# Stream turns moved from the first gate pass to the output stage; ScalarE evicts queries ahead of the Gelu

## The chip, the core and the metric

The kernel runs on one core of a Trainium2 chip, in float32. The metric is the device time of one execution in microseconds (us), lower is better.

## The reference, cut to what matters

One layer of a hybrid encoder over 384 tokens: a prompt of 256 (two tiles of 128) and eight running streams of 16 tokens, which make one tile.

```python
xn = rmsnorm(x)                                  # (tokens, 2048)
qA, kA, vA, qB, kB, vB, f, gA, gB = split(xn @ w_in)
m  = sigmoid(gA) * (yA @ w_br_a) + sigmoid(gB) * (yB @ w_br_b)   # yA, yB: two attentions
h  = x + m @ w_out
q  = rmsnorm(h) @ w_pq                           # 8 heads x 2 halves x 128
s  = q . sub_keys                                # 128 scores for each half
# top 16 of each half, top 16 of their 256 sums -> 128 experts of a token, idx and gate
a  = peer_u[idx] . rmsnorm(h)                    # a row of 2048 floats for each expert
y  = h + sum(gelu(a) * gate * peer_v[idx])       # and another such row
```

With 128 experts of each token, a tile of 128 tokens needs 128 gathers of 128 rows from `peer_u`, 1 MB each, and as many from `peer_v`.

## The kernel before

**Two fronts.** The part up to the scores s is a front. The streams' front runs first, then the prompt's; while the prompt's front runs (TensorE works for it), the streams' experts are worked off beside it on GpSimd (gathers) and VectorE (arithmetic).

**Stream turns.** The streams' 128 experts are 32 turns of 4 slots, and a half is 2 slots. For each slot `expert_turn` makes a dot with a gathered row of `peer_u` (L1490) and adds the row of `peer_v` that belongs to the slot one turn earlier (L1480). Between two turns stands a Gelu on ScalarE (L877) and a small product with the gates (L1471), which waits for it. The rows of u have 2 buffers, those of v have 4: GpSimd issues the next gather (L492) when the dot or the add has freed a buffer. The 64 halves are dealt out by hand along the prompt's front: `HALVES` in its attention groups, `PASS_HALVES` in its four gate passes (so many before the pass's products, so many behind them), one behind each of four output chunks and two behind the root, and `QUERY_HALVES` in the four query chunks. ScalarE runs the same deal, since its Gelus lie in its own program between the front's evictions.

**The prompt's front behind its attention.** A gate pass i is three chunks of weights (gate A, gate B, branches), a chunk being 4 pieces of 1 MB in a ring of four buffers (`wring`); the gates of pass 0 have been multiplied already within the last attention group, so that pass 0 holds the branches alone. VectorE multiplies gates and branches (L1311) and adds the two (L1316), TensorE turns the result (L756), and the next pass begins. The output stage is four chunks of `w_out`: VectorE adds x and scales (L1326, L1333), TensorE turns it (L773) behind the next chunk. Then comes the root of the second norm: ScalarE squares (L1020), places the last turned chunk (L1011) and takes the square root (L871), and VectorE finishes rstd and writes `xn2` (L1338), the normed h that the prompt's dots will read. The query stage is four chunks of `w_pq`; its first two pieces are multiplied before the last turn of h. For each chunk, ScalarE evicts it with rstd as scale (L1048), runs the Gelus of `QUERY_HALVES`, places the turned queries (L1033) and evicts the key scores (L1038).

**Picking.** `pick` finds a prompt tile's experts in four parts of 9 steps (top 8 twice of both halves, sums, top 8 twice, places, two lookups, name) and a finish. Part i of the first tile needs the scores of query chunk i, and the first 32 gathers of the tile need part 0. Before the change three steps follow each slot of the third query turn and of the last four adds (`last_rows`), which makes 24; the rest lies between the prompt's dots, two steps for each nine dots.

**The prompt's experts.** GpSimd gathers 256 u-tiles into six buffers, of which two lie outside the weight ring and four are the ring's (L533); VectorE makes 256 dots (L1541). Behind them the first halves of the v rows are worked off by dense products on TensorE and the second halves by gathers.

SP loads all weight pieces in order: a piece is issued when TensorE is through with the one that lay in its buffer (`piece_done`).

Of the kernel before, what the change touches and what calls it, by code (L numbers as in the profile page):

```python
# [18 lines left out]
NCH = D // CW  # L19
# [11 lines left out]
TURN = 4  # L31
# [10 lines left out]
PASS_HALVES = (4, 3)  # L42
# [145 lines left out]
def build(nc, a):  # L188

    with ExitStack() as ctx:  # L190
# [201 lines left out]
        def _(pool):  # L392
# [132 lines left out]
            for k in range(2 * SLOTS):  # L525
# [3 lines left out]
                if k == 2:  # L529
                    pool.wait_ge(R.pq_read, 2 * NCH)  # L530
# [334 lines left out]
        def _(act):  # L865
# [35 lines left out]
            def front(F, experts):  # L901
# [91 lines left out]
                for i in range(NCH):  # L993
                    for s in range(2):
# [5 lines left out]
                        experts(PASS_HALVES[0] // 2)  # L1000
# [4 lines left out]
                    experts(PASS_HALVES[1])  # L1005
# [8 lines left out]
                for i in range(NCH):  # L1014
                    if i:
                        place_h(i - 1)
                    experts(1)
# [7 lines left out]
                experts(2)  # L1025

                def keys(i):
                    for t in range(n):
                        u = n * i + t
                        act.wait_ge(F.pq_turned, u + 1)  # L1030
                        if i:
                            act.wait_ge(F.key_done, n * i)
                        act.activation(F.pqT[:, :, t * P:(t + 1) * P], blocks(6 + u % 2), ACT.Copy  # L1033
                                       ).then_inc(F.pq_placed, 1)
                    for t in range(n):
# [6 lines left out]
                for i in range(NCH):  # L1042
                    act.wait_ge(piece_done, F.after(PQ + i))
                    for t in range(n):
                        if i:
                            act.wait_ge(F.pq_turned, n * (i - 1) + t + 1)
                        act.wait_ge(F.xn2_ready, t + 1)
                        act.activation(stage[:, t, :], ps[:, 2 * (i % 2) + t, :], ACT.Copy,  # L1048
                                       scale=rstd[:, 1, t0 + t:t0 + t + 1]).then_inc(F.pq_read, 1)
                    experts(QUERY_HALVES[i])  # L1050
                    keys(i)
# [100 lines left out]
        def _(dve):  # L1152
# [53 lines left out]
            def front(F, experts, between=None):  # L1206
# [99 lines left out]
                for i in range(NCH):  # L1306
                    experts(PASS_HALVES[0])
# [11 lines left out]
                    experts(PASS_HALVES[1])  # L1319

                dve.wait_ge(F.x_again, 16)
                for i in range(NCH):
# [159 lines left out]
            def expert_turn(E, tau, xn, h, first=False, slots=range(TURN), between=None):  # L1482
# [4 lines left out]
                for s in slots:  # L1487
# [6 lines left out]
                    if between:  # L1494
                        between()
# [19 lines left out]
            def stream_turns(halves, between=None):  # L1515

                for tau, half in streams_place.next(halves):
                    expert_turn(ES, tau, S.xn2[:, 0, :], S.h[:, 0, :], first=streams_place.first(tau),
                                slots=range(half * TURN // 2, (half + 1) * TURN // 2), between=between)
# [5 lines left out]
            def pick_steps():  # L1525

                for _ in range(3):
                    stages.pop(0)()

            front(R, stream_turns, pick_steps)  # L1530
# [44 lines left out]
            for k in range(2 * SLOTS):  # L1575
                dot(k)
                if k == SLOTS + 1:
# [97 lines left out]
```

## Time and profile before

| what | us |
|---|---|
| median of 3 runs | 2933.37 (2932.15 to 2935.93) |
| the profiled execution, its own time | 2943.72 |
| its span in the trace | 2941.8 |
| VectorE busy | 1909.7 |
| TensorE busy (matmul) | 2120.5 |
| DMA moved | 1047.10 MB, mean 356 GB/s |

The profiled execution is 10.35 us over the median of the runs, and 1.9 us of it lie outside the span. Times of the trace below are in us from the start of the span. The prompt's gate passes end at about 1437, its output stage at 1563, its query stage at 1713; the dots begin at 1737 and end at 2403.

### The profile page before, as it was taken

The numbers are of one execution on the slowest core, as the hardware profiler recorded it, in microseconds if no ns is written. First come the engines' busy times: TensorE is split into PE (matmuls) and PEld (weight loads), VectorE is DVE, ScalarE is ACT, GpSimd is POOL, SyncE is SP. The second block draws the span as 40 slices with busy tenths as digits, with TensorE's granted clock in tenths as the row PEclk, the third lists the DMA queues.
The fourth block names the chain that finished last, engine by engine and source line by source line (L and its number), as shares of the span: only waits on it lengthen the run. The fifth ranks groups of instructions, "written<-read, shape, count | busy, mean of one in ns | idle before, by whom it ended". The sixth has DMA issues, their size and how long they took to land.

```text
span 2941.8 us, 19523 instructions
## 1 busy us (share of the span) xinstructions
PE 2120.5 (72%) x6070; PEld 1074.1 (37%) x6070; DVE 1909.7 (65%) x2627; ACT 470.9 (16%) x1104; POOL 1241.2 (42%) x854
## 2 busy tenths in 40 slices
PE   7999999999999978878888820000232027999997
PEld 3665444444545533333334410000231015444443
DVE  1212000276686877557545799999999998666666
ACT  1212100112222211001001000000795025000000
POOL 2000000014253455335324437777777875444444
PEclk9999999999999989989999965555555557999998
DMA  9777688869799999899988969999999997999999
GB/s 356 265 287 256 230 285 300 300 222 397 287 405 372 407 412 411 340 401 362 395 315 352 409 247 396 397 400 398 393 402 400 413 377 246 409 408 407 409 409 361
DMA packets 271464, 1047.10 MB, mean 356 GB/s; under 512 B 19856, under 2 KB 19856, under 8 KB 203280
## 3 DMA queue, kind: packets, MB, share of 16 engines
q0 software_dynamic: 113792, 697.85, 59.5%
q1 hardware_dynamic: 154880, 343.97, 32.4%
q10 hardware_dynamic: 2704, 4.21, 0.4%
q8 instruction: 43, 0.70, 0.1%
q14 instruction: 45, 0.37, 0.0%
HBM read 1036.50 MB, written 9.45 MB: 356 GB/s over the span
## 4 chain that ended last, share of the span: by engine, by line
DVE 26%; DMA 24%; PE 10%; issue 6%; POOL 4%; ACT 0%; POOLq 0%; DVEq 0%; SPq 0%; ACTq 0%
DVE bigr L1541 13%; DMA yTr<-in_peer_v,fold 11%; PE ps L562 10%; DMA bigr<-in_w_br_b 4%; DVE spare L1541 3%; DMA bigr<-in_w_in 3%; DVE hr L1571 3%; DMA bigs<-in_peer_u,idxnow 2%; POOL bigr L533 2%; DMA bigs<-in_peer_v,idxnow 2%; DMA bigr<-in_peer_v,fold 2%; DVE pwork L1352 1%; DMA bigr<-in_w_out 1%; DVE bigs L1480 1%; DVE normed L1561 1%
## 5 line engine op out<-in xcount | busy, mean ns | idle before, releaser
L562 PE MATMUL ps<-bigr 128*128 128x512 f32 x1920 | 859.6, 606 | 40.9 <-DMA bigr<-in_w_in 21.4
L562 PEld LDWEIGHTS ps<-bigr 128*128 128x128 f32 x1920 | 368.4, 195 | 492.3 <-issue 440.6
L1541 DVE SCALAR_TENSOR_TENSOR bigr<-bigr 128x2048 f32<-128x2048 f32 x213 | 478.1, 2288 | 6.5 <-DMA bigr<-in_peer_u,fold 5.3
L533 POOL DMA_INDIRECT bigr<-in_peer_u,fold x213 | 412.3, 1936 | 133.3 <-DVE bigr L1541 68.5
L492 POOL DMA_INDIRECT bigs<-in_peer_u,idxnow x128 | 213.5, 1668 | 559.4 <-DVE bigs L1490 539.1
L562 PE MATMUL ps<-bigr,bigs 128*128 128x512 f32 x896 | 407.6, 610 | 21.0 <-DMA bigr<-in_w_in 17.4
L1571 DVE SCALAR_TENSOR_TENSOR hr<-yTr,fold,hr 128x1024 f32<-128x1024 f32 x205 | 263.2, 1284 | 132.3 <-DMA yTr<-in_peer_v,fold 129.9
L1480 DVE SCALAR_TENSOR_TENSOR bigs<-bigs,acts 128x2048 f32<-128x2048 f32 x128 | 300.9, 2350 | 69.3 <-DMA bigs<-in_peer_v,idxnow 69.2
L1490 DVE SCALAR_TENSOR_TENSOR bigs<-bigs 128x2048 f32<-128x2048 f32 x128 | 293.3, 2291 | 78.2 <-DMA bigs<-in_peer_u,idxnow 77.4
L543 POOL DMA_INDIRECT yTr<-in_peer_v,fold x205 | 206.6, 1008 | 224.2 <-DVE hr L1571 214.3
L562 PEld LDWEIGHTS ps<-bigr,bigs 128*128 128x128 f32 x896 | 171.3, 196 | 219.9 <-issue 213.0
L492 POOL DMA_INDIRECT bigs<-in_peer_v,idxnow x128 | 223.7, 1748 | 54.0 <-issue 39.6
L827 PE MATMUL ps<-ident,fold 128*128 128x128 f32 x2 | 1.0, 476 | 297.1 <-DVE fold L1547 297.1
L851 PE MATMUL ps<-spare,bigs 128*128 128x512 f32 x384 | 180.5, 592 | 0.7 <-ACT bigr L1123 0.7
L851 PE MATMUL ps<-spare,bigr 128*128 128x512 f32 x384 | 180.4, 592 | 0.0
L821 PE MATMUL ps<-ident,fold 128*128 128x128 f32 x4 | 1.4, 446 | 224.8 <-DVE fold L1438 224.8
L1311 DVE TENSOR_TENSOR bigr<-ps,bigr 128x512 f32<-128x512 f32 x24 | 15.7, 687 | 213.8 <-PE ps L562 213.8
L562 PE MATMUL ps<-bigr,yTr 128*128 128x512 f32 x256 | 121.5, 634 | 37.3 <-DMA bigr<-in_w_br_a 23.2
L839 PE MATMUL ps<-normed,bigr 128*128 128x128 f32 x256 | 65.5, 437 | 101.6 <-issue 93.6
L533 POOL DMA_INDIRECT spare<-in_peer_u,fold x43 | 86.2, 2004 | 57.2 <-DVE spare L1541 47.1
L478 POOL IOTA fold<- 128x128 f32 x1 | 0.2, 238 | 258.9 <-DVE stage L1333 258.9
L827 PEld LDWEIGHTS ps<-ident,fold 128*128 128x128 f32 x2 | 0.4, 183 | 297.9 <-DVE fold L1547 297.9
(254 smaller groups left out, 2195.2 us busy)
## 6 DMA issues: line engine op xcount, KB each, us to landing
bigr<-in_w_in SPq DMA_DIRECT2D x160, 1024.0 KB, 6.1
spare<-in_peer_v SPq DMA_DIRECT2D x96, 512.0 KB
bigr<-in_w_out SPq DMA_DIRECT2D x32, 1024.0 KB, 6.9
bigr<-in_w_pq SPq DMA_DIRECT2D x32, 1024.0 KB, 6.1
bigr<-in_w_br_a SPq DMA_DIRECT2D x16, 1024.0 KB
bigr<-in_w_br_b SPq DMA_DIRECT2D x16, 1024.0 KB, 10.9
bigr<-in_peer_v SPq DMA_DIRECT2D x32, 512.0 KB
bigr<-in_ckT_a POOLq DMA_DIRECT2D x2, 2048.0 KB, 10.4
```

The source lines that it names most:

```text
L492: pool.indirect_dma_start(row, None, table[:, :], bass.IndirectOffsetOnAxis(ap=col, axis=0)).then_inc(loaded, 16)
L533: pool.indirect_dma_start(ER.urow[k % UBUF], None, a["peer_u"][:, :], bass.IndirectOffsetOnAxis(ap=eidx[t][:, s:s + 1], axis=0)).then_inc( ...
L543: pool.indirect_dma_start(ER.vrow[k % VBUF], None, halves, bass.IndirectOffsetOnAxis(ap=hidx[:, t, s:s + 1], axis=0)).then_inc(ER.v_loaded ...
L562: last = mm(ps[:, bank + t, :], src[:, k0 + k, t * P:(t + 1) * P], wring[:, s, k, :], start=(k0 + k == 0), stop=(k0 + k == kt - 1))
L839: last = mm(ps[:, 4 + b, n * P:(n + 1) * P], hot_a[t][:, b, n, :], hot_i[:, b, n, :], start=(n == 0), stop=True, **sk)
L851: last = mm(ps[:, 2 * t + c, :], table[t][:, i, :], ER.dense[b][:, c * CW:(c + 1) * CW], start=(i == 0), stop=(i == P - 1))
L1352: step(dve.max_index(x[:, lo:lo + 8], v_[:, lo:lo + 8], w))
L1480: dve.scalar_tensor_tensor(h, E.vrow[s], acts[:, s:s + 1], h, ALU.mult, ALU.add).then_inc(E.v_free, 1)
L1490: dve.scalar_tensor_tensor(E.urow[u], E.urow[u], 1.0, xn, ALU.mult, ALU.mult, accum_out=dots[:, s:s + 1]).then_inc(E.u_free, 1)
L1541: dve.scalar_tensor_tensor(ER.urow[u], ER.urow[u], 1.0, R.xn2[:, t, :], ALU.mult, ALU.mult, accum_out=rdots[:, t, s:s + 1]).then_inc(ER.u_ ...
L1561: dve.tensor_tensor(hot_i[:, b, :, :], column(0), grid, ALU.is_equal).then_inc(ER.i_hot, 1)
L1571: dve.scalar_tensor_tensor(h, ER.vrow[v], gates[t][:, s:s + 1], h, ALU.mult, ALU.add).then_inc(ER.v_free, 1)
```

## The change

The deal of the stream turns is altered. Pass 0 has 2 halves before its products and 3 behind them, where it had 4 and 3. Each of the first three output chunks is followed by two halves (a whole turn), where each of four chunks was followed by one; so six halves lie before the root, where four did. The turn behind the root stands before the writing of `xn2` and no longer behind it. On ScalarE the evictions of a query chunk wait for rstd instead of `xn2`, and they and the placing of the turned queries stand ahead of the stream's Gelu. The picking steps leave the third query turn: 12 still go with the last adds, then 6 follow at once, and 9 follow the second dot. The prompt's third to sixth gather each wait for the piece of the last query chunk that lay in their buffer, and no longer for all evictions of the queries.

```diff
-PASS_HALVES = (4, 3)
+PASS_HALVES = ((2, 3), (4, 3), (4, 3), (4, 3))
+OUT_HALVES = (2, 2, 2, 2)
@@ gpsimd
-                if k == 2:
-                    pool.wait_ge(R.pq_read, 2 * NCH)
+                if 2 <= k < UBUF:
+                    pool.wait_ge(piece_done, R.after(PQ + NCH - 1, k - 2))
@@ scalar
                 for i in range(NCH):
                     if i:
                         place_h(i - 1)
-                    experts(1)
+                    if i < NCH - 1:
+                        experts(OUT_HALVES[i])
...
                 root(rstd[:, 1, t0:t0 + n])
-                experts(2)
...
-                        act.wait_ge(F.xn2_ready, t + 1)
+                        act.wait_ge(F.rstd_ready, 2)
                         act.activation(stage[:, t, :], ps[:, 2 * (i % 2) + t, :], ACT.Copy,
                                        scale=rstd[:, 1, t0 + t:t0 + t + 1]).then_inc(F.pq_read, 1)
+                    if i == 0:
+                        experts(OUT_HALVES[NCH - 1])
+                    place_query(i)
                     experts(QUERY_HALVES[i])
-                    keys(i)
+                    read_keys(i)
@@ vector
                 for i in range(NCH):
-                    experts(PASS_HALVES[0])
+                    experts(PASS_HALVES[i][0])
...
-                    experts(1)
+                    if i < NCH - 1:
+                        experts(OUT_HALVES[i])
                 dve.wait_ge(F.h_squared, n)
                 root(rstd[:, 1, t0:t0 + n], ssq[:, 1, t0:t0 + n], nwork[:, t0:t0 + n], D)
+                dve.sem_inc(F.rstd_ready, 1)
+                experts(OUT_HALVES[NCH - 1])
                 for t in range(n):
                     dve.scalar_tensor_tensor(F.xn2[:, t, :], F.h[:, t, :], rstd[:, 1, t0 + t:t0 + t + 1], ln2b,
                                              ALU.mult, ALU.mult).then_inc(F.xn2_ready, 1)
-                experts(2)
                 for i in range(NCH):
-                    experts(QUERY_HALVES[i], between if i >= 2 else None)
+                    experts(QUERY_HALVES[i])
...
             last_rows(ES, TURNS, S.h[:, 0, :], pick_steps)
+            pick_steps(6)
             finish_first = stages.pop()
...
             for k in range(2 * SLOTS):
                 dot(k)
+                if k == 1:
+                    pick_steps(9)
```

VectorE at the root, before: the end of the half behind the last output chunk, the root, `xn2` (bigr<-hr,rstd,spare) and the first row of the next turn.

```order
L1480 SCALAR_TENSOR_TENSOR bigs<-bigs,acts 128x2048 [waits v_free_s,v_loaded3_s]
L1169 TENSOR_SCALAR ssq<-ssq 128x2 [waits h_squared_r]
L1170 RECIPROCAL rstd<-ssq 128x2 [waits dve_order]
L1173 TENSOR_TENSOR nwork<-rstd 128x2 [waits root_done]
L1174 TENSOR_TENSOR nwork<-nwork,ssq 128x2 [waits dve_order]
L1175 TENSOR_SCALAR nwork<-nwork 128x2 [waits dve_order]
L1176 TENSOR_TENSOR rstd<-rstd,nwork 128x2 [waits dve_order]
L1338 SCALAR_TENSOR_TENSOR bigr<-hr,rstd,spare 128x2048 [waits dve_order]
L1338 SCALAR_TENSOR_TENSOR bigr<-hr,rstd,spare 128x2048
L1471 TENSOR_TENSOR acts<-gelu,gates_s 128x4 [waits v_free_s,gelu_done_s]
L1490 SCALAR_TENSOR_TENSOR bigs,dots<-bigs 128x2048 [waits u_loaded0_s,acts_ready_s]
```

The same place now, from the last step of the root on. Here bigs,dots<-bigs is a dot and bigs<-bigs,acts an add.

```order
L1182 TENSOR_TENSOR rstd<-rstd,nwork 128x2 [waits dve_order]
L1479 TENSOR_TENSOR acts<-gelu,gates_s 128x4 [waits dve_order,v_free_s,gelu_done_s]
L1498 SCALAR_TENSOR_TENSOR bigs,dots<-bigs 128x2048 [waits u_loaded0_s,acts_ready_s]
L1488 SCALAR_TENSOR_TENSOR bigs<-bigs,acts 128x2048 [waits v_free_s,v_loaded0_s]
L1498 SCALAR_TENSOR_TENSOR bigs,dots<-bigs 128x2048 [waits u_loaded1_s]
L1488 SCALAR_TENSOR_TENSOR bigs<-bigs,acts 128x2048 [waits v_free_s,v_loaded1_s]
L1498 SCALAR_TENSOR_TENSOR bigs,dots<-bigs 128x2048 [waits u_loaded0_s]
L1488 SCALAR_TENSOR_TENSOR bigs<-bigs,acts 128x2048 [waits v_free_s,v_loaded2_s]
L1498 SCALAR_TENSOR_TENSOR bigs,dots<-bigs 128x2048 [waits u_loaded1_s]
L1488 SCALAR_TENSOR_TENSOR bigs<-bigs,acts 128x2048 [waits v_free_s,v_loaded3_s]
L1347 SCALAR_TENSOR_TENSOR bigr<-hr,rstd,spare 128x2048 x2
L1479 TENSOR_TENSOR acts<-gelu,gates_s 128x4 [waits v_free_s,gelu_done_s]
```

A whole turn stands between rstd and `xn2`, and none between the last output chunk and the root.

ScalarE from the root's square root into the first query chunk, before (stage<-ps,rstd is the eviction of a query chunk, normed<-ps the placing, yTr<-ps the eviction of key scores):

```order
L871 ACTIVATE rstd<-rstd 128x2 [waits ss_ready]
L877 ACT_TABLE_LOAD [waits acts_ready_s]
L877 ACTIVATE gelu<-dots 128x4 [waits u_free_s]
L1048 ACTIVATE stage<-ps,rstd 128x512 [waits xn2_ready_r,piece_done,k_stored_r]
L1048 ACTIVATE stage<-ps,rstd 128x512 [waits xn2_ready_r]
L877 ACTIVATE gelu<-dots 128x4 [waits acts_ready_s,u_free_s]
L1033 ACTIVATE normed<-ps 128x4x128 [waits pq_turned_r] x2
L1038 ACTIVATE yTr<-ps 128x512 [waits key_done_r] x2
```

And now:

```order
L872 ACTIVATE rstd<-rstd 128x2 [waits ss_ready]
L1051 ACTIVATE stage<-ps,rstd 128x512 [waits rstd_ready_r,piece_done,k_stored_r]
L1051 ACTIVATE stage<-ps,rstd 128x512 [waits rstd_ready_r]
L878 ACT_TABLE_LOAD [waits acts_ready_s]
L878 ACTIVATE gelu<-dots 128x4 [waits u_free_s]
L1034 ACTIVATE normed<-ps 128x4x128 [waits pq_turned_r] x2
L878 ACTIVATE gelu<-dots 128x4 [waits acts_ready_s,u_free_s]
L1041 ACTIVATE yTr<-ps 128x512 [waits key_done_r] x2
```

The two evictions have passed one Gelu, the placing has passed the next one, and the wait for `xn2` is gone from them.

## Rows read from the trace of the kernel before

**Rows 1.** The page: span, then busy and DMA share in 40 slices.

```profile
span 2941.8 us, 19523 instructions
...
PE   7999999999999978878888820000232027999997
...
DVE  1212000276686877557545799999999998666666
...
DMA  9777688869799999899988969999999997999999
```

**Rows 2.** Windows, core 0: stretch, its length, busy of PE, PEld, DVE, ACT, POOL; clock, DMA, GB/s.

```profile
1440.00:1690.00 250.00, 224.85 (x571) 104.79 (x570) 158.53 (x174) 20.46 (x36) 103.81 (x64) 0.95 0.92 361
1600.00:1690.00 90.00, 73.22 (x203) 37.09 (x204) 69.14 (x96) 8.63 (x17) 42.96 (x28) 0.91 1.02 411
1690.00:1750.00 60.00, 19.67 (x70) 10.89 (x68) 58.27 (x153) 7.29 (x12) 17.13 (x12) 0.69 0.58 220
```

**Rows 3.** Timeline of VectorE, pass 0: start us, us, instruction, [idle before it, releaser].

```profile
1070.63 0.16 DVE L1471 TENSOR_TENSOR acts<-gelu,gates_s 128x4 f32<-128x4 f32 x1
...
1096.90 2.48 DVE L1311 TENSOR_TENSOR bigr<-ps,bigr 128x512 f32<-128x512 f32 x4
1099.42 1.29 DVE L1316 TENSOR_TENSOR stage<-bigr 128x512 f32<-128x512 f32 x2
...
1100.82 2.29 DVE L1490 SCALAR_TENSOR_TENSOR bigs<-bigs 128x2048 f32<-128x2048 f32 x1
1103.04 2.35 DVE L1480 SCALAR_TENSOR_TENSOR bigs<-bigs,acts 128x2048 f32<-128x2048 f32 x1
1105.30 2.28 DVE L1490 SCALAR_TENSOR_TENSOR bigs<-bigs 128x2048 f32<-128x2048 f32 x1
```

**Rows 4.** Timeline of TensorE, from pass 0 to pass 2.

```profile
1057.40 29.40 PE L562 MATMUL ps<-bigr,yTr 128*128 128x512 f32 x64 [3.25 <-ACT bigr L998]
1100.16 1.97 PE L756 MATMUL ps<-ident,stage 128*128 128x128 f32 x8 [13.37 <-DVE stage L1316]
...
1214.57 1.97 PE L756 MATMUL ps<-ident,stage 128*128 128x128 f32 x8 [2.11 <-DVE stage L1316]
...
1327.05 1.92 PE L756 MATMUL ps<-ident,stage 128*128 128x128 f32 x8 [2.11 <-DVE stage L1316]
```

**Rows 5.** Timeline of TensorE, the query stage.

```profile
1577.46 1.04 PE L773 MATMUL ps<-ident,stage 128*128 128x128 f32 x8
...
1607.62 1.97 PE L578 MATMUL ps<-ident,stage 128*128 128x128 f32 x8 [8.52 <-ACT stage L1048]
...
1632.99 3.79 PE L793 MATMUL ps<-fold,normed 128*128 128x128 f32 x16 [9.17 <-ACT normed L1033]
```

**Rows 6.** Timeline of VectorE, from the root to the third query turn.

```profile
1581.58 4.61 DVE L1338 SCALAR_TENSOR_TENSOR bigr<-hr,rstd,spare 128x2048 f32<-128x2048 f32 x2
...
1610.15 0.16 DVE L1471 TENSOR_TENSOR acts<-gelu,gates_s 128x4 f32<-128x4 f32 x1
...
1635.69 0.17 DVE L1471 TENSOR_TENSOR acts<-gelu,gates_s 128x4 f32<-128x4 f32 x1
...
1663.85 0.16 DVE L1471 TENSOR_TENSOR acts<-gelu,gates_s 128x4 f32<-128x4 f32 x1
...
1667.39 2.35 DVE L1480 SCALAR_TENSOR_TENSOR bigs<-bigs,acts 128x2048 f32<-128x2048 f32 x1 [0.86 <-DMA bigs<-in_peer_v,idxnow]
```

**Rows 7.** The chain that ended last: start us, us, what.

```profile
1469.14 28.31 DMA bigr<-in_w_out
...
1736.90 2.30 DVE spare L1541 x2
```

**Rows 8.** Timeline of GpSimd, the prompt's third gather.

```profile
1710.45 0.94 POOL L533 DMA_INDIRECT bigr<-in_peer_u,fold  x1 [6.43 <-ACT stage L1048]
```

**Rows 9.** Timeline of VectorE, the prompt's dots with and without picking left.

```profile
2214.41 2.29 DVE L1541 SCALAR_TENSOR_TENSOR bigr<-bigr 128x2048 f32<-128x2048 f32 x1
...
2216.62 2.29 DVE L1541 SCALAR_TENSOR_TENSOR bigr<-bigr 128x2048 f32<-128x2048 f32 x1
...
2342.59 2.29 DVE L1541 SCALAR_TENSOR_TENSOR bigr<-bigr 128x2048 f32<-128x2048 f32 x1 [0.19 <-DMA bigr<-in_peer_u,fold]
...
2345.09 2.29 DVE L1541 SCALAR_TENSOR_TENSOR bigr<-bigr 128x2048 f32<-128x2048 f32 x1 [0.19 <-DMA bigr<-in_peer_u,fold]
```

**Rows 10.** Waits of VectorE, 1740 to 2420: who for whom, us, times, longest.

```profile
DVE bigr L1541 <- DMA bigr<-in_peer_u,fold: 5.3, 25, 0.8
DVE spare L1541 <- DMA spare<-in_peer_u,fold: 0.9, 5, 0.2
```

More of the change, by code:

```diff
@@ L999, in front @@
                                            ).then_inc(F.proj_read, 1)
-                        experts(PASS_HALVES[0] // 2)
+                        experts(PASS_HALVES[i][0] // 2)
                     for t in range(n):
@@ L1004, in front @@
                                        ).then_inc(F.m_placed, 1)
-                    experts(PASS_HALVES[1])
+                    experts(PASS_HALVES[i][1])
                 def place_h(i):
@@ L1024, in front, with place_query @@
                 root(rstd[:, 1, t0:t0 + n])
-                experts(2)
-                def keys(i):
+                def place_query(i):
                     for t in range(n):
@@ L1034, in keys, with read_keys @@
                                        ).then_inc(F.pq_placed, 1)
+                def read_keys(i):
                     for t in range(n):
@@ L1204, in forget_gate, with front @@
                                          ALU.subtract).then_inc(F.lf_ready, 1)
-            def front(F, experts, between=None):
+            def front(F, experts):
                 n, t0 = F.n, F.tiles[0]
@@ L1318, in front @@
                     dve.sem_inc(F.mix_read, 2 * n)
-                    experts(PASS_HALVES[1])
+                    experts(PASS_HALVES[i][1])
                 dve.wait_ge(F.x_again, 16)
@@ L1480, in add_row, with expert_turn @@
                 dve.scalar_tensor_tensor(h, E.vrow[s], acts[:, s:s + 1], h, ALU.mult, ALU.add).then_inc(E.v_free, 1)
-            def expert_turn(E, tau, xn, h, first=False, slots=range(TURN), between=None):
+            def expert_turn(E, tau, xn, h, first=False, slots=range(TURN)):
                 NU = len(E.urow)
@@ L1493, in expert_turn @@
                         add_row(E, tau, s, h)
-                    if between:
-                        between()
             def last_rows(E, tau, h, between):
@@ L1513, in _, with stream_turns @@
             streams_place = Place()
-            def stream_turns(halves, between=None):
+            def stream_turns(halves):
                 for tau, half in streams_place.next(halves):
                     expert_turn(ES, tau, S.xn2[:, 0, :], S.h[:, 0, :], first=streams_place.first(tau),
-                                slots=range(half * TURN // 2, (half + 1) * TURN // 2), between=between)
+                                slots=range(half * TURN // 2, (half + 1) * TURN // 2))
             part_at = D // NCH
@@ L1523, in _, with pick_steps @@
             stages = pick(R, 1, cand_at, onehot_at, NCH)
-            def pick_steps():
-                for _ in range(3):
+            def pick_steps(count=3):
+                for _ in range(count):
                     stages.pop(0)()
-            front(R, stream_turns, pick_steps)
+            front(R, stream_turns)
             assert TURNS == streams_place.turns
             last_rows(ES, TURNS, S.h[:, 0, :], pick_steps)
+            pick_steps(6)
             finish_first = stages.pop()
```

## The prediction

> **What bounds the kernel now.** The page comes first. TensorE is near full until slice 24, VectorE is at nine tenths for ten slices behind that, and the share of DMA falls below nine tenths only in places [rows 1]. So no one engine bounds the program. The question for each stage is whether DMA has idle time in it, since the change neither adds nor drops a byte: it moves rows of experts from one stage to another.
>
> The windows show where that idle time lies. Between 1600 and 1690 DMA moves 411 GB/s at a full share; I take this as the ceiling. Over 1440 to 1690 the mean is 361, so (411 - 361) x 250 us = 12.5 MB, or 30.4 us of DMA, are missing there. The next 60 us run at 220 GB/s [rows 2]. One row is 1.048 MB, which is 2.55 us at 411.
>
> The timelines then tell what waits. In pass 0 TensorE is through with the branches at 1086.80 (1057.40 + 29.40) and then sits idle for 13.37 us until VectorE adds the gates at 1099.42: VectorE was still in its four halves until 1096.90 [rows 3, 4]. In passes 1 and 2 the same idle time is 2.11 us, and a pass lasts 114.4 (1100.16 to 1214.57) and 112.5 us (to 1327.05) [rows 4]. In the output stage the chain names a weight piece that took 28.31 us to come [rows 7], so the stream's rows and the weights compete at its start. In the query stage TensorE waits twice for ScalarE, 8.52 and 9.17 us [rows 5], but DMA is full behind 1600 [rows 2], so this wait isn't what ends the stage. From 1667 on VectorE has nearly no gap: its last wait of the stage is 0.86 us [rows 6], and from 1740 to 2420 its waits for rows come to 6.2 us in 30 times [rows 10].
>
> **The change, part by part.** I follow one point, the end of the prompt's dots. Behind it nothing changes, and the 10.35 us between the profiled execution and the median, and what lies outside the span, are carried over as they are.
>
> *Pass 0, four halves to two: -13.1.* The first two halves were over when the gates' product of the next turn began, at 1070.63 [rows 3]. Then VectorE is free before TensorE is done, and the products follow TensorE: the second pair of products starts at about 1086.9 instead of 1098.1 (half of the 2.48 us behind 1096.90), and the addition stands at 1088.2 instead of 1099.42. That is 11.2 us. VectorE then goes into the next seven halves with all six row buffers full, as before pass 2, so I give pass 1 the length of pass 2: another 1.9. Bounds: 9 if the weights are late because ScalarE and VectorE change places somewhere, and 20.4 (8 rows x 2.55) if the whole DMA time of the rows comes back.
>
> *Output stage, 8 rows more before the query turns: -2.0.* They need 20.4 us of DMA in a stretch that lacks 30.4. A chunk of weights with a whole turn is 4 + 8 pieces of 1 MB, 30.6 us of DMA, against about 28 us of TensorE, so in three chunks TensorE gets late by some 2 to 3 us each. Then VectorE has nothing to do from the last output chunk to the root, and DMA catches up with the weights in that gap. The root itself can't come earlier than the last turn of h on TensorE (1577.46), which stands behind two pieces of query weights [rows 5]. Some idle time will stay: I take 8 us, so that 22.4 of the 30.4 are used and the end of the stage's bytes moves by 20.4 - 22.4. Bounds: all of it used, -10.0, and none, +20.4. I stand near the first since TensorE is the only other claim on the stretch and has four pieces in store.
>
> The turn ahead of `xn2` costs nothing: the write of `xn2` is 4.61 us [rows 6] wherever it stands, and nobody reads it before the dots once ScalarE's evictions don't wait for it. Ahead of the Gelu, ScalarE's evictions take away TensorE's 8.52 and 9.17 us [rows 5]. I cost that at nothing: the cover is the full DMA behind 1600, through which the same bytes must still pass.
>
> *Third query turn without picking: +6.7.* The turn before it took 25.5 us (1610.15 to 1635.69) at the pace of DMA. VectorE's own work in four slots is 4 x 4.48 = 17.9 us (dot to dot, 1100.82 to 1105.30 [rows 3]). Before, picking filled the gaps of the third turn, and only 0.86 us were lost [rows 6]. Now 25.5 - 17.9 - 0.9 = 6.7 us are idle, and the picking comes later in full. Bounds: 1.6 (two rows a slot at 2.55 with no weights beside them) and 7.6 (nothing was saved by picking).
>
> *Later picking for the gathers: 0.* From 1663.85 [rows 6] to the first dot at 1736.90 [rows 7] are 73.1 us; less 17.9 for the slots, 4 x 2.26 for the adds and 0.9 of waiting, 45.2 us are left for 24 steps, 1.9 each. The prompt's first gather needs nine steps. They are now over 23 to 24 us behind the end of the turns, and nine more steps and an add, some 19 us, lie between them and the first dot. Six rows need 15.3 us. The wait for its own buffer spares the third gather 6.43 us [rows 8], which nobody needs. If this cover were gone, a dot would wait up to 5 us.
>
> *Fewer steps beside the dots: +3.9.* Two steps in nine dots keep VectorE at the pace of DMA. A dot alone takes 2.21 us (2214.41 to 2216.62), but when picking is over it is 2.49 or 2.50 (2342.59 to 2345.09) with a wait for each row [rows 9]. Before, 48 steps are dealt out, to dot 216, and of the last 40 dots 30 wait [rows 10]. Now nine steps go at once and 45 are dealt out, to dot 202; 14 more dots run at 2.49, 14 x 0.28 = 3.9. Bounds: 0 and 3.9.
>
> *Sum:* -11.2 - 1.9 - 2.0 + 6.7 + 3.9 = -4.5 us. Against the profiled execution's own 2943.72 that is 2939.2; against the median 2933.37 it is **2928.9**.
>
> *A rule that speaks against it.* The windows show 411 GB/s over 90 us [rows 2]. The Trainium skill, page "DMA: Bandwidth & Descriptors", section "Bandwidth", says that for transfers from HBM the side of the HBM binds at about 358 GB/s for a core. By that figure 1440 to 1690 had no room, and the eight rows would cost 23.4 us, an estimate from the page, where I have -2.0; the sum would be +20.9 us. The trace doesn't agree with the figure here, so I keep the sum.
>
> **Rivals.**
> - *The output stage doesn't take the rows (slower).* Its first chunks already wait for weights [rows 7]. If a whole turn in each chunk starves TensorE and the room appears only later, in the gap before the root, where no buffer is free to use it, then perhaps a quarter of the 30.4 us is used: +12.8 instead of -2.0, a sum of +10.3, 2943.7. It decides against the change from less than 10 us used (a sum over +5.9). The full stream in 1600 to 1690 speaks for it, the mean of 361 against it. 0.18. The skill's rule above is the extreme of this case.
> - *The trade cancels.* Pass 0 gives its 11.2 and pass 1 nothing, and the output stage gives nothing: -11.2 + 0 + 6.7 + 3.9 = -0.6, 2932.8. 0.20.
> - *DMA uses nearly all of the gap.* With the queries evicted early, the weights of the last chunks are in before the third query turn, which runs at two rows a slot: +1.6 for +6.7; and the stage keeps 2.4 us of idle time, -7.6 for -2.0. Sum -15.2, 2918.2. That DMA is full from 1600 on speaks for it; that it needs both VectorE and TensorE never to be late speaks against it. 0.20.
> - *The forecast*, -10 to 0 (2923 to 2933): 0.42.
>
> **How the numbers follow.** A change of 0.2% (5.9 us) is about what a measurement can tell from none. The case in which DMA uses nearly all of the gap is faster (0.20), and so is half of the forecast's own: 0.41. The other half and the case that cancels are the same: 0.41. The slower rival leaves 0.18. The range goes from 2916, a little below the fast rival, to 2942, just under the slower one's middle.
>
> **What would show it.** In the trace after: TensorE's idle time before the first L756 near 2 us and that instruction at about 1089; pass 1 about 112.5 long; the window from the passes' end to the last turn over 380 GB/s; no wait of TensorE for ScalarE's evictions in the query stage; VectorE with 6 to 7 us of waits in the third query turn; some 44 waits at the end of the dots. I am wrong if the last turn of h comes more than 10 us later behind pass 3 than now, if the products of pass 0 wait for something other than TensorE, or if a Gelu, which now stands behind the placing of the queries, holds VectorE: that needs TensorE to be later in the query stage than before.

## The result, and the profile after

The changed kernel takes **2944.35 us** (median of 8 runs, 2940.62 to 2949.28) against 2932.92 us of the kernel before on the same chips (8 runs, 2927.36 to 2938.32): a ratio of **1.0038, 95% interval 1.0026 to 1.0049**. It is slower by 11 us, where -4.5 was forecast, and outside the range.

The two profiled executions don't show that. Their spans are 2940.6 and 2941.8 us, almost the same. The execution that was profiled before was a long one of its kernel; the one of after is typical (its own time is 2942.52). What the trace can give is therefore the lengths of the stages, and these need more than one trace. The experiments below supply them.

The page after, its span and its DMA row, as in [rows 1]:

```profile
span 2940.6 us, 19518 instructions
...
DMA  9777788869799989999999959999999997999999
```

Counted from 0, slices 20 and 21 of DMA are 9 where they were 8, and slice 23 is 5 where it was 6: idle time has gone from the output stage, and some has come where the prompt's gathers start.

Windows after (stretch, its length, busy of PE, PEld, DVE, ACT and POOL, clock, DMA share, GB/s). The first is the stretch of [rows 2] set back with the start of the stage, the second the ceiling again, the third lies before the first dot:

```profile
1420.00:1670.00 250.00, 224.59 (x569) 103.08 (x567) 165.85 (x131) 21.64 (x39) 116.76 (x73) 0.97 0.97 384
1580.00:1670.00 90.00, 79.45 (x221) 38.32 (x219) 64.09 (x45) 10.78 (x20) 45.31 (x31) 0.96 1.02 410
1680.00:1710.00 30.00, 10.84 (x44) 5.89 (x43) 29.03 (x104) 5.68 (x9) 8.38 (x6) 0.78 0.31 111
```

The stage moves 384 GB/s instead of 361. (411 - 384) x 250 us are 6.75 MB, or 16.4 us of DMA, that are still missing; 8 had been taken. Before the first dot, DMA moves 111 GB/s.

Where in the stage does DMA have idle time? The first two windows are of the kernel before, the next three of the changed one; the stage begins at 1437.52 and at 1417.70:

```profile
1440.00:1507.00 67.00, 59.54 (x136) 25.85 (x135) 38.26 (x32) 0.61 (x3) 30.14 (x18) 0.95 0.96 376
1507.00:1600.00 93.00, 92.10 (x234) 41.85 (x232) 51.14 (x48) 11.22 (x17) 30.71 (x18) 1.00 0.80 301
```

```profile
1420.00:1447.00 27.00, 27.00 (x64) 11.97 (x63) 19.86 (x16) 0.21 (x1) 19.84 (x10) 1.00 0.97 377
1447.00:1524.00 77.00, 62.14 (x141) 26.78 (x140) 48.41 (x39) 1.70 (x5) 32.69 (x22) 0.93 1.02 410
1524.00:1580.00 56.00, 56.00 (x149) 26.01 (x148) 33.48 (x34) 8.96 (x13) 18.92 (x12) 1.00 0.82 311
```

Before, the first two chunks (to 1507) run at 376 GB/s, nearer the ceiling; of the 30.4 us that the prediction found missing, about 25 lie behind them ((411 - 301) x 93 us). The changed kernel fills its second and third chunk to 410 GB/s, where TensorE then waits, and still leaves the fourth chunk and what follows at 311.

TensorE after, from pass 0 to the end of the passes, the rows that answer to [rows 4]:

```profile
1054.84 29.40 PE L563 MATMUL ps<-bigr,yTr 128*128 128x512 f32 x64 [3.25 <-ACT bigr L999]
1086.35 1.26 PE L757 MATMUL ps<-ident,stage 128*128 128x128 f32 x8 [2.11 <-DVE stage L1322]
...
1198.13 1.72 PE L757 MATMUL ps<-ident,stage 128*128 128x128 f32 x8 [2.11 <-DVE stage L1322]
...
1308.69 1.26 PE L757 MATMUL ps<-ident,stage 128*128 128x128 f32 x8 [2.11 <-DVE stage L1322]
...
1417.70 1.26 PE L757 MATMUL ps<-ident,stage 128*128 128x128 f32 x8 [2.11 <-DVE stage L1322]
```

The idle time ahead of the first L757 is 2.11 us, where it was 13.37, and no longer than in the other passes: the products follow TensorE. The next passes are 111.8, 110.6 and 109.0 us long.

TensorE after, output and query stage, as [rows 5]:

```profile
1464.66 15.70 PE L563 MATMUL ps<-bigr 128*128 128x512 f32 x32 [3.55 <-DMA bigr<-in_w_out]
...
1483.41 7.11 PE L563 MATMUL ps<-bigr 128*128 128x512 f32 x16 [2.18 <-DMA bigr<-in_w_out]
1493.32 7.13 PE L563 MATMUL ps<-bigr 128*128 128x512 f32 x16 [2.81 <-DMA bigr<-in_w_out]
1502.24 7.13 PE L563 MATMUL ps<-bigr 128*128 128x512 f32 x16 [1.78 <-DMA bigr<-in_w_out]
1513.91 9.92 PE L563 MATMUL ps<-bigr 128*128 128x512 f32 x16 [4.54 <-DMA bigr<-in_w_out]
...
1566.62 1.04 PE L774 MATMUL ps<-ident,stage 128*128 128x128 f32 x8
...
1623.43 1.97 PE L579 MATMUL ps<-ident,stage 128*128 128x128 f32 x8 [5.04 <-ACT stage L1051]
```

The second output chunk waits for weights once (1464.66), the third before each of its four pieces (1483.41 to 1513.91). The last turn of h is at 1566.62, 148.9 us behind the end of pass 3 (139.9 before). In the query stage one of the two waits for ScalarE is gone and the other is 5.04 us, where none was forecast.

All waits of TensorE between these two points, then the chain that ended last, which goes through the same weights:

```profile
PE ps L563 <- DMA bigr<-in_w_out: 14.9, 5, 4.5
```

```profile
1440.75 23.87 DMA bigr<-in_w_out
...
1480.60 33.28 DMA bigr<-in_w_out
...
1720.60 2.30 DVE spare L1548 x2
```

A wait can cost more than itself. The piece behind the longest one takes 9.92 us, where the piece before it takes 7.13, and the granted clock of its stretch is 0.72 of full speed on the mean, so that TensorE was on the lower of its two levels (1.2 GHz) for a part of it:

```profile
1513.90:1524.00 10.10, 10.09 (x20) 4.51 (x21) 0.13 (x1) 0.00 (x0) 0.00 (x0) 0.72 1.02 396
```

VectorE after, third query turn, as [rows 6]; its waits from there to the first dot (who for whom, us, times, longest); and the prompt's first gathers on GpSimd, as [rows 8]:

```profile
1650.74 0.16 DVE L1479 TENSOR_TENSOR acts<-gelu,gates_s 128x4 f32<-128x4 f32 x1
...
1659.32 2.29 DVE L1498 SCALAR_TENSOR_TENSOR bigs<-bigs 128x2048 f32<-128x2048 f32 x1 [2.20 <-DMA bigs<-in_peer_u,idxnow]
...
1677.94 0.16 DVE L1479 TENSOR_TENSOR acts<-gelu,gates_s 128x4 f32<-128x4 f32 x1
```

```profile
DVE bigs L1488 <- DMA bigs<-in_peer_v,idxnow: 5.0, 6, 1.0
DVE bigs L1498 <- DMA bigs<-in_peer_u,idxnow: 4.7, 4, 2.2
```

```profile
1702.07 2.93 POOL L534 DMA_INDIRECT spare<-in_peer_u,fold  x1 [20.37 <-DVE fold L1446]
...
1723.17 2.75 POOL L534 DMA_INDIRECT spare<-in_peer_u,fold  x1 [11.95 <-DVE spare L1548]
```

The turn takes 27.2 us. Of the 9.7 us of waits, 0.96 belong to the last row of the turn before; 8.8 us lie in the turn and the first add behind it. In the kernel before they are 1.1 us, the 0.86 of [rows 6] and this one:

```profile
1664.22 2.29 DVE L1490 SCALAR_TENSOR_TENSOR bigs<-bigs 128x2048 f32<-128x2048 f32 x1 [0.21 <-DMA bigs<-in_peer_u,idxnow]
```

The first gather waits 20.37 us for picking. But the first dot, at 1720.60 (the chain above), waits for no row: six gathers have gone out by 1711, and the seventh waits for VectorE's first dot, until 1723.17.

The waits at the end of the dots, as [rows 10]:

```profile
DVE bigr L1548 <- DMA bigr<-in_peer_u,fold: 7.3, 36, 0.8
DVE spare L1548 <- DMA spare<-in_peer_u,fold: 1.3, 7, 0.2
```

They are 43 and not 30.

### The profile page after: what moved, and what is told of

It reads as the page before. It is cut to its first block, busy times and chain, and to the rows that moved or that the text cites. A ratio compares the mean times of both kernels' runs of the same rounds, so it can differ in the third digit from the quotient of the medians.

```text
span 2940.6 us, 19518 instructions
## 1 busy us (share of the span) xinstructions
PE 2114.4 (72%) x6070; PEld 1065.9 (36%) x6070; DVE 1910.7 (65%) x2627; ACT 468.1 (16%) x1102; POOL 1255.8 (43%) x854
## 4 chain that ended last, share of the span: by engine, by line
DMA 25%; DVE 25%; PE 11%; issue 5%; POOL 4%; ACT 0%; POOLq 0%; DVEq 0%; SPq 0%; ACTq 0%
DVE bigr L1548 12%; PE ps L563 10%; DMA yTr<-in_peer_v,fold 10%; DMA bigr<-in_w_br_b 4%; POOL bigr L534 3%; DVE hr L1578 3%; DVE spare L1548 3%; DMA bigr<-in_peer_v,fold 3%; DMA bigs<-in_peer_u,idxnow 2%; DMA bigr<-in_w_in 2%; DMA bigr<-in_w_out 2%; DMA bigs<-in_peer_v,idxnow 2%; DVE pwork L1360 1%; POOL spare L534 1%; DVE normed L1568 1%
## 5 line engine op out<-in xcount | busy, mean ns | idle before, releaser
L493 POOL DMA_INDIRECT bigs<-in_peer_v,idxnow x128 | 232.4, 1816 | 44.5 <-issue 41.2
## 6 DMA issues: line engine op xcount, KB each, us to landing
bigr<-in_ckT_a POOLq DMA_DIRECT2D x2, 2048.0 KB, 10.6
```

The costliest lines, as they stand in the source:

```text
L493: pool.indirect_dma_start(row, None, table[:, :], bass.IndirectOffsetOnAxis(ap=col, axis=0)).then_inc(loaded, 16)
```

## Experiments

Eleven kernels were run, each timed in 5 rounds beside the kernel before. "Part alone" means the kernel before with that part of the change. All ratios are to the kernel before, with a 95% interval.

### e1: the kernel before, again

No edit.

> The kernel before, unchanged. It is there for a second trace and for how far two equal kernels fall apart. Theory A (the two traces are typical, and the 10 us between the profiled execution and the median of the kernel before lie evenly over the program): the new trace has the same stages as the old one within 3 us, the own time of its execution again lies about 10 us over the median. Theory B (the profiled execution of the kernel before was slow by chance in one stage, and the true kernel reaches the end of the prompt's dots some 10 us earlier than 2402.6): the new trace shows that stage shorter by about 10 us. Ratio to the kernel before: 1.000 within 0.15% by both.

Measured: 1.0011 (0.9999 to 1.0024), 2937.23 us over 12 runs; its profiled execution 2939.72. So two equal kernels fell 0.1% apart here, and 0.15% is what a ratio of these can tell. The stages of its trace stand in the table below: the passes are 3.9 us longer than in the first trace and the output stage 5.8 us shorter. Neither theory is quite right. Stages of the same code differ by 5 us from one execution to the next, and the first trace had a long output stage. The window that answers to the first of [rows 2], and the wait of TensorE in the output stage, both of this second trace:

```profile
1442.00:1692.00 250.00, 228.91 (x583) 106.57 (x581) 165.77 (x187) 20.72 (x38) 103.31 (x65) 0.96 0.94 369
```

```profile
PE ps L562 <- DMA bigr<-in_w_out: 3.8, 2, 3.0
```

369 GB/s instead of 361: (411 - 369) x 250 us are 25.5 us of DMA missing and not 30.4. The room that the prediction counted on was partly a feature of one execution.

### e2: the deal of the turns alone

The halves behind the four output chunks are taken from a table, which had been one each.

```diff
-PASS_HALVES = (4, 3)
+PASS_HALVES = ((2, 3), (4, 3), (4, 3), (4, 3))
+OUT_HALVES = (2, 2, 2, 0)
```

> The kernel before with the new deal of stream turns alone: 2 and 3 halves in pass 0, two halves behind each of the first three output chunks, the turn behind the root still behind xn2, picking, ScalarE's order and the gathers' waits as before. Theory 1 (the terms of the prediction, with the sizes read from the trace after): the passes give 17.3 us, the output stage takes 9.0, so -8 us, ratio 0.997. Theory 2 (the output stage takes more than the passes give, by far more in timed executions than in the profiled one): 0 to +12 us, ratio 1.000 to 1.004.

Measured: 0.9992 (0.9977 to 1.0008), that is -2 us, -7 to +2. The -15.1 of the prediction for its two terms is out, and so, narrowly, is the -8 that I had read from the single pair of traces. It stands just under the second theory's range. TensorE's waits for output weights in its trace:

```profile
PE ps L563 <- DMA bigr<-in_w_out: 12.7, 4, 4.4
```

### e3: the move of the picking alone

```diff
-                    experts(QUERY_HALVES[i], between if i >= 2 else None)
+                    experts(QUERY_HALVES[i])
...
             last_rows(ES, TURNS, S.h[:, 0, :], pick_steps)
+            pick_steps(6)
...
                 dot(k)
+                if k == 1:
+                    pick_steps(9)
```

> The kernel before with the move of the picking steps alone: none in the third query turn, 12 with the last adds, 6 behind them, 9 behind the second dot. Theory 1 (terms of the prediction): VectorE idles 6.7 us more in the third query turn and 3.9 us more at the end of the dots, +10.6 us, ratio 1.0036. Theory 2 (the picking is neutral, since DMA runs ahead of VectorE when it isn't held up by picking): within 3 us, ratio 0.999 to 1.001.

Measured: 1.0041 (1.0025 to 1.0056), +12 us (7 to 16), where the terms sum to 10.6: the first theory. This part alone is as slow as the whole change. Its waits at the end of the dots:

```profile
DVE bigr L1542 <- DMA bigr<-in_peer_u,fold: 7.4, 37, 0.8
DVE spare L1542 <- DMA spare<-in_peer_u,fold: 1.3, 7, 0.2
```

44 waits and 8.7 us, against 30 and 6.2 [rows 10], which is the last term of the prediction.

### e4: the order at the root and on ScalarE alone

On ScalarE:

```diff
                 root(rstd[:, 1, t0:t0 + n])
-                experts(2)
...
-                        act.wait_ge(F.xn2_ready, t + 1)
+                        act.wait_ge(F.rstd_ready, 2)
...
+                    if i == 0:
+                        experts(2)
+                    place_query(i)
                     experts(QUERY_HALVES[i])
-                    keys(i)
+                    read_keys(i)
```

and on VectorE the turn behind the root ahead of `xn2`.

> The kernel before with the order at the root and in the query stage alone: the turn behind the root ahead of xn2, ScalarE's query evictions wait for rstd and stand ahead of the Gelus, as does the placing. Theory 1: TensorE loses its 17.7 us of waits for ScalarE, but DMA bounds the stage, -2 to 0 us, ratio 0.9993 to 1.000. Theory 2 (a Gelu behind the placing holds VectorE, or the earlier weights take DMA from the stream's rows and nothing comes back): +3 to +8 us, ratio 1.001 to 1.003.

Measured: 1.0004 (0.9989 to 1.002). Level, as the first theory has it, though the interval (-3 to +6 us) doesn't shut out the low end of the second.

### e5: the same deal, with the extra rows later in the output stage

```diff
-OUT_HALVES = (2, 2, 2, 0)
+OUT_HALVES = (1, 2, 2, 1)
```

> As e2_deal, but with 1, 2, 2 and 1 halves behind the four output chunks instead of 2, 2, 2 and 0. In the traces of e2_deal and after, the output stage is 9 to 12 us longer than in those with the old deal, and TensorE waits for weights in the second and third chunk. Theory 1 (the extra rows starve TensorE at the stage's start, where the ring is still empty from the last pass; later there is room): the stage from the last turn of pass 3 to the last turn of h is 136 to 141 us, as before, and the time is 6 to 10 us under e2_deal, ratio to the kernel before 0.996 to 0.997. Theory 2 (eight rows cost their DMA time wherever they stand): stage 145 to 149 us, ratio as e2_deal, 0.998 to 1.000.

Measured: **0.9949 (0.9932 to 0.9966)**, -15 us: the first theory, and by more than it said. Six halves lie before the root in both, and the weights and rows are the same; only their place in the stage differs. TensorE's waits for weights up to the last turn of h, the output stage itself, and three windows (250 us behind the passes, the first chunk, and from there to 1570), from its trace:

```profile
PE ps L563 <- DMA bigr<-in_w_out: 2.8, 2, 1.7
PE ps L563 <- DMA bigr<-in_w_pq: 2.3, 1, 2.3
```

```profile
1468.99 14.39 PE L563 MATMUL ps<-bigr 128*128 128x512 f32 x32 [1.73 <-DMA bigr<-in_w_out]
...
1485.28 27.71 PE L563 MATMUL ps<-bigr 128*128 128x512 f32 x64 [1.02 <-DMA bigr<-in_w_out]
...
1513.69 27.72 PE L563 MATMUL ps<-bigr 128*128 128x512 f32 x64
...
1542.12 7.03 PE L563 MATMUL ps<-bigr 128*128 128x512 f32 x16
1551.41 7.11 PE L563 MATMUL ps<-bigr 128*128 128x512 f32 x16 [2.25 <-DMA bigr<-in_w_pq]
1558.35 1.04 PE L774 MATMUL ps<-ident,stage 128*128 128x128 f32 x8
```

```profile
1425.00:1675.00 250.00, 226.97 (x579) 105.50 (x579) 183.36 (x196) 20.68 (x37) 115.88 (x74) 0.96 1.01 400
1424.00:1452.00 28.00, 27.90 (x61) 12.29 (x62) 20.64 (x16) 0.25 (x2) 17.73 (x11) 0.94 0.96 376
1452.00:1570.00 118.00, 112.39 (x284) 50.59 (x283) 79.67 (x71) 11.84 (x19) 45.23 (x30) 1.00 1.01 400
```

The waits are 5.1 us, where e2 has 12.7 and the changed kernel 14.9. The third and fourth chunk run without a stop, the stage takes 136.2 us (1422.15 to 1558.35), and DMA moves 400 GB/s to its end, where the changed kernel falls to 311. From the changed kernel's trace to this one the stage is 12.7 us shorter: 9.8 us of it are waits, and about 3 are TensorE's own work, 130.4 us and not 133.5, at a mean granted clock of 0.99 over the stage and not 0.97.

### e6: only the idle time in the third query turn

```diff
-                    experts(QUERY_HALVES[i], between if i >= 2 else None)
+                    experts(QUERY_HALVES[i])
...
             last_rows(ES, TURNS, S.h[:, 0, :], pick_steps)
+            pick_steps(12)
```

> The kernel before with no picking in the third query turn; those twelve steps follow behind the last adds, so that 24 steps lie before the first dot and 48 beside the dots, as before. Only the idle time of the third turn is changed. Theory 1 (e3_picks is the sum of two terms, 6.7 us of idle time in the third turn and 3.9 us of more waits at the end of the dots): +6.7 us, ratio 1.0023, 29 or 30 waits at the end of the dots. Theory 2 (it is the late first gather, which starts the dots behind): the dots' first rows are waited for by more than 3 us and the ratio is as e3_picks, 1.004.

Measured: 1.0017 (1.0002 to 1.0032), +5 us. Its waits from the third turn to the first dot, and those at the end of the dots:

```profile
DVE bigs L1480 <- DMA bigs<-in_peer_v,idxnow: 5.2, 6, 1.0
DVE bigs L1490 <- DMA bigs<-in_peer_u,idxnow: 4.1, 4, 1.5
```

```profile
DVE bigr L1542 <- DMA bigr<-in_peer_u,fold: 5.5, 25, 0.8
DVE spare L1542 <- DMA spare<-in_peer_u,fold: 0.9, 5, 0.2
```

Of the 9.3 us, 0.87 belong to the row before the turn; 8.5 us against 1.1 lie in it, and the end of the dots is as before. It stands with the sum of two terms. The interval reaches from 0.6 to 9.4 us and overlaps that of e3, so that the size of the term is known better from the waits than from the time.

### e7: the changed kernel with the picking put back

The edit is e3's, taken back in the changed kernel.

> The changed kernel with the picking put back: three steps with each slot of the third query turn, 12 with the last adds, 48 beside the dots. The deal, the order and the gathers' waits as changed. Theory 1 (the picking is the whole loss of the change, and the other parts add up to e2_deal and e4_order): ratio to the kernel before 0.9985 to 1.0005, about 11 us under the changed kernel. Theory 2 (the parts act on each other, so that the picking costs little once the deal is new): ratio 1.002 to 1.004.

Measured: 0.9985 (0.9968 to 1.0003). It is in the range of the first theory. Without the picking's move, the rest of the change is level or a little faster (-9 to +1 us).

### e8: the two halves of pass 0 in the query stage

One half is behind each output chunk, as before, and picking stands beside the third query turn only.

```diff
+PASS_HALVES = ((2, 3), (4, 3), (4, 3), (4, 3))
-QUERY_HALVES = (2, 2, 2, 0)
+QUERY_HALVES = (2, 2, 2, 2)
```

> The kernel before with pass 0 at 2 and 3 halves, the output stage at one half behind each chunk as before, and the two halves behind the fourth query chunk instead (no picking beside them). It moves the same eight rows to where DMA is already full. Theory 1 (rows cost 2.55 us each where DMA is full, and the passes give back 11 to 17 us): +4 to +9 us, ratio 1.001 to 1.003. Theory 2 (where the rows stand doesn't matter, only that pass 0 is shorter): ratio as e2_deal, 0.998 to 1.000. The passes alone tell what pass 0 gives: from the start of its branches to the last turn of pass 3 about 362 us, against 373 to 384 with the old deal.

Measured: 1.0022 (1.0007 to 1.0037), +6.5 us. From the last turn of h to the first dot its trace has 178.5 us, where the first trace has 159.4: 19 us for eight rows, near the 20.4 that they take of DMA. So rows cost their full DMA time where DMA is full, as the first theory has it, and pass 0 gives back some 14 us. The interval just touches that of e2; against e5 it is clear that the place of the rows matters.

### e9, e10, e11

e9 is e5 with the order of e4 and the gathers' waits; e10 is the whole change with e5's deal; e11 is the gathers' waits alone:

```diff
-                if k == 2:
-                    pool.wait_ge(R.pq_read, 2 * NCH)
+                if 2 <= k < UBUF:
+                    pool.wait_ge(piece_done, R.after(PQ + NCH - 1, k - 2))
```

> As e5_deal_late, with ScalarE's order, the turn ahead of xn2 and the gathers' waits of the changed kernel added; the picking as before. Theory 1 (these edits are worth nothing, since e4_order was level and e7_no_picks stood at e2_deal): ratio to the kernel before 0.993 to 0.997, as e5_deal_late. Theory 2 (TensorE's waits for ScalarE in the query stage, 8 to 9 us each, count once the output stage no longer starves): 0.990 to 0.993.

> The changed kernel with one edit: 1, 2, 2 and 1 halves behind the output chunks instead of 2, 2, 2 and none. Theory 1 (the terms add: the deal in its better place -15 us, the picking +12, the order 0): ratio to the kernel before 0.998 to 1.000, 13 us under the changed kernel. Theory 2 (what is gained before the root is lost to the picking, because the prompt's gathers start late anyway): 1.002 to 1.004.

> The kernel before with the gathers' waits alone: the third to sixth gather of the prompt wait for their own buffer's weight piece and not for the evictions of the queries. Theory 1: the third gather goes out some 6 us earlier and no dot waited for it, 0 us, ratio 0.999 to 1.001. Theory 2 (DMA's idle time before the dots is worth something later, since the dots' end waits for DMA): -3 to -6 us, ratio 0.998 to 0.999.

Measured: e9 0.9962 (0.9944 to 0.998), e10 0.9995 (0.9976 to 1.0013), e11 0.9993 (0.9978 to 1.0008). All three are in the first theory's range. e10 differs from the changed kernel by one table of numbers and takes back its whole loss (its interval is -7 to +4 us). e5 and e9 both beat both kernels; their intervals overlap, and e5 is the simplest. The deal (1, 2, 2, 1) beats (2, 2, 2, 0) in three pairs that differ in it alone: e5 and e2 by 13 us, e10 and the changed kernel by 13, e9 and e7 by 7. The last pair alone would not be clear of noise.

### The stages in all traces

Worked out from one trace each (starts of the same rows as in [rows 4] to [rows 6] and the first and last dot), in us. Passes: from the start of pass 0's branches to the turn of pass 3. Output: from there to the last turn of h. Query: to the first dot. Dots: to the start of the last dot.

| kernel | passes | output | query | dots | ratio |
|---|---|---|---|---|---|
| before | 380.1 | 139.9 | 159.4 | 663.5 | 1 |
| e1, the same | 384.0 | 134.1 | 157.9 | 662.7 | 1.0011 |
| e11, gathers | 379.5 | 134.2 | 158.0 | 663.7 | 0.9993 |
| e4, order | 377.8 | 133.4 | 158.3 | 663.5 | 1.0004 |
| e6, picks idle | 379.9 | 135.6 | 165.2 | 663.1 | 1.0017 |
| e3, picks | 373.2 | 136.6 | 153.8 | 678.1 | 1.0041 |
| the changed kernel | 362.9 | 148.9 | 154.0 | 677.7 | 1.0038 |
| e2, deal | 362.6 | 147.0 | 159.0 | 663.1 | 0.9992 |
| e7, no picks | 369.6 | 148.8 | 156.9 | 663.6 | 0.9985 |
| e8, deal to query | 365.9 | 141.6 | 178.5 | 663.2 | 1.0022 |
| e5, deal late | 366.7 | 136.2 | 157.0 | 663.0 | 0.9949 |
| e9, late and order | 360.3 | 143.1 | 158.1 | 663.5 | 0.9962 |
| e10, late and all | 364.1 | 135.8 | 154.7 | 678.0 | 0.9995 |

From the start of the last dot to the end of the span all thirteen have 541.4 to 545.2 us.

Passes and output stage trade with each other from trace to trace (e9 has 360.3 and 143.1, e5 366.7 and 136.2), so their sum says more: 514.7 us on the mean of the six traces with the old deal, 513.2 of the three with the change's, 502.1 of the three with (1, 2, 2, 1), and 507.5 in e8.

## Why the prediction was wrong

**Pass 0, -13.1: right.** The six traces with four halves in pass 0 have a mean of 379.1 us for the passes, the seven with two halves 364.6: -14.5. The second pair of products waits for TensorE as was said, and TensorE's idle time ahead of the turn fell from 13.37 to 2.11 us.

**Output stage, 8 rows more, -2.0: this is the step that failed.** With the change's deal the stage takes 148.2 us (mean of three traces), with the old deal 135.6 (mean of six): +12.6. The error is 14.6 of the 15.7 us between the forecast sum and the measured 11.2 (0.38% of 2933). e8, with the old deal in this stage and the new one in pass 0, has 141.6, so a part of the +12.6 may come with the earlier end of the passes. The sum of both stages doesn't hang on this: -15.1 was forecast and -1.5 measured, and e2 by its time gives -2. Three things in the step were wrong.

First, the gap was read as one sum over 250 us. I took it that idle DMA anywhere in the stretch would be filled by rows issued anywhere in it. But of its 30.4 us about 25 lie behind the second chunk (376 GB/s before 1507, 301 behind it). The first six pieces of the changed kernel's stage still run without a wait for weights; then a whole turn behind each of the first two chunks takes DMA from weights that TensorE needs at once. Its waits for weights are 14.9, 12.7 and 13.2 us (e7) in the three traces with the change's deal and 2.3 to 7.5 in the six with the old. Behind the last output chunk no half is dealt out, and DMA has room again that nobody uses (311 GB/s).

Second, the lateness was foreseen and taken as free. The prediction has TensorE late by 2 to 3 us in each of three chunks and lets DMA catch up in the gap before the root. But the root stands behind the last turn of h, and this behind all four chunks on TensorE: what TensorE has waited isn't given back. The waits came to 14.9 us in the changed kernel where 6 to 9 were foreseen, and TensorE's work at the lower clock added some 3 us to them, held against e5.

Third, the size of the gap was that of one execution: 30.4 us in the trace shown, 25.5 in the next. The rows were bound to be dearer by some of that.

e5 shows that it is the place: the same six halves as 1, 2, 2, 1 bring the waits to 5.1, the stage to 136.2 and the time down by 13 us against e2. It moves one half away from the start and one into the gap before the root; which of the two counts more wasn't separated. In e9, with the same deal, the waits are 10.0 us and the stage 143.1, so e5's trace is a good one of its kind; the sum of passes and stage is the same within 1 us in both.

The sign "over 380 GB/s" in the window from the passes to the last turn came true (384 over 250 us from 1420), while the stage got longer. A fuller DMA was no sign of a faster stage.

**The rival was the case.** "The output stage doesn't take the rows" had +12.8 for this term and 2943.7 us in all, and gave weight to the first chunks' waits for weights. The measured stage gives +12.6, the time 2944.35. The mechanism is the one that it names; that both numbers agree within 1 us is luck, since it took "perhaps a quarter" of the gap as used, and traces of one deal differ by 6.5 us in this stage. It had 0.18. (By the prediction's own sum this rival decides against the change from less than 12 us used, and not from less than 10: 20.4 - 12.0 = 8.4, and 8.4 - 13.1 + 10.6 = 5.9.) The chain's 28 us of a weight piece [rows 7] should have had more weight than the mean of a long window.

**Third query turn, +6.7: right, if a little small.** The waits rose by 7.7 us in the changed kernel and by 7.4 in e6, at the upper bound of 7.6 or just over it; the time of e6 is +5 (0.6 to 9.4). **Fewer steps beside the dots, +3.9: right** in count (43 and 44 waits where 44 were forecast). The waits rose by 2.4 and 2.5 us. A dot that waits also loses the 0.08 us by which it would overlap the one before (2.29 us long, 2.21 apart [rows 9]); over 14 dots that makes 3.6 in all. The two together are 10.6, and e3 measured +12 (7 to 16). So the picking is the part that makes the kernel slower, and the deal only failed to pay for it.

**ScalarE's order, `xn2`, the gathers, 0: right as far as it can be told.** e4 and e11 are level, within -3 to +6 and -6 to +2 us. No Gelu held VectorE in the query stage. The late first gather cost nothing, since the first dot had its row.

**The comparison by one profiled execution.** The forecast was made against a span of 2941.8, and the changed kernel's is 2940.6. Read alone, the pair would say that the change is neutral, as would its stages: -17.2 in the passes, +9.0 in the output stage. The spans say -1.2 and the timed runs +11.2. Half of this difference lies in two stages of the pair, held against the means of the same deals: the passes were 1.0 and the output stage 4.3 us longer in the first trace than on the average, the passes 1.7 shorter and the output stage 0.7 longer in the second, 6.3 us in all. The rest wasn't traced to a stage.

## What to carry to other kernels

Idle DMA in a window is room only for transfers that can be issued in the same few microseconds: look at its slices beside the waits of the engine that shares the DMA engines, and put moved work where that engine has its buffers full, not where it has just been starved. An engine that starves early in a chain of dependent work doesn't get the time back from room that opens later. Work that fills the gaps of a transfer-bound phase (here the picking) is cheaper there than elsewhere: twelve steps of about 1.9 us, moved behind the last adds in e6, brought the waits up by 7.4 us. Such work should be the last thing to be moved out. Where stages of the same code differ by 5 us between executions, a term of a few us is read from several traces.

## What was not expected of the hardware

The same kernel took 2926.7 to 2942.1 us in 30 runs, at a granted clock of 0.847 to 0.853. Six traces with the same deal differ by 10.8 us in the passes and by 6.5 in the output stage, while the dots, bound by VectorE, came out at 662.7 to 663.7 us in all traces without the picking's move. Long executions tend to have the lower clock: of 32 other runs of this kernel, the 13 at 0.847 or less have a median of 2942.9 us, the 9 at 0.850 or more 2932.6. Whether the clock makes them long or the waits of a long one lower its clock is open.

With weights and rows in flight together, the two queues came forward by equal numbers of packets, as if they took turns. Over 20 us of the changed kernel's output stage (1440 to 1460), q0 with the gathered rows and q1 with the weights (packets, MB, share of 16 engines) have:

```profile
q0 software_dynamic: 891, 6.51, 78.6%
q1 hardware_dynamic: 890, 1.78, 23.5%
```

The kernel before has 896 and 895 from 1460 to 1480. But the packets of rows are nearly all of 8192 bytes and those of weights of 2048, so that the weights get 89 GB/s of 415. A piece of 1.048 MB then comes each 11.8 us, where TensorE needs 6.9 us for it. In the passes of the changed kernel its pieces start 11.6 to 12.1 us apart (1140.08, 1151.88, 1163.51, 1175.63), in the third output chunk up to 11.7 (1502.24 to 1513.91). The weights' share beside the rows, and not the rate of DMA, set TensorE's pace there. Weights in larger packets would be the next thing to try; no run here does.
